# Gated attention in a two-block kernel: stacked halves of queries and keys, products with tokens on partitions, gates applied after the products

## What is computed

```python
def _masked_softmax(s, mask):
    s = jnp.where(mask, s.astype(jnp.float32), -1e30)
    m = jnp.max(s, axis=-1, keepdims=True)
    e = jnp.exp(s - m) * mask
    return e / jnp.maximum(jnp.sum(e, axis=-1, keepdims=True), 1e-30)

    # per block of 128 queries
        s = jnp.einsum('bqghd,bngd->bghqn', qb, k_cmp) * scale
        p_cmp = _masked_softmax(s - slopes * dist, dist >= 0)
        o_cmp = jnp.einsum('bghqn,bngd->bqghd', p_cmp.astype(v_cmp.dtype), v_cmp)
        ...
        s = jnp.einsum('bqghd,bgqmd->bghqm', qb, k_sel) * scale
        p = _masked_softmax(s - slopes * dist, dist >= 0)
        o_slc = jnp.einsum('bghqm,bgqmd->bqghd', p.astype(v_sel.dtype), v_sel)
        ...
        p = _masked_softmax(s - slopes * wd.astype(jnp.float32), wmask)
        o_win = jnp.einsum('bghqk,bkgd->bqghd', p.astype(vw.dtype), vw)
        o = gb[..., 0:1] * o_cmp + gb[..., 1:2] * o_slc + gb[..., 2:3] * o_win
```

## Times and profile before

| | |
|---|---|
| median of 3 runs | 2704.24 us (2703.32 to 2704.76) |
| the profiled execution | 2705.93 us, span 2704.1 us |
| PE busy | 2589.8 us, 96% of the span |
| DVE, ACT, POOL busy | 1299.0, 821.7, 1163.7 us |
| mean granted PE clock | 0.973 |
| first attention | about 190 to 492 us of the span |

### The profile page before, as it was taken

One profiled execution on the slowest core, in us unless ns is written; L12 is line 12 of the kernel. 1 busy time (PEld: TensorE's weight loads), 2 busy tenths in 40 slices (PEclk: granted clock), 3 DMA queues, 4 the chain that ended last, 5 costly groups with the idle time before them and its releaser, 6 DMA issues.

```text
span 2704.1 us, 37833 instructions
## 1 busy us (share of the span) xinstructions
PE 2589.8 (96%) x12935; PEld 2185.8 (81%) x12935; DVE 1299.0 (48%) x2419; ACT 821.7 (30%) x1458; POOL 1163.7 (43%) x564
## 2 busy tenths in 40 slices
PE   7969998899999999999999999999999999999998
PEld 5757877788788888789988888887899888888877
DVE  5578887566443222137776532221277765322211
ACT  2234555567321110024444321100144444211101
POOL 4742221000047777850000287778700001877786
PEclk8878998999999999999999999999999999999999
DMA  6320000233333333232223233333322232333332
GB/s 128 86 47 17 9 15 14 73 94 86 86 91 93 98 96 94 87 94 81 75 63 89 83 93 98 96 91 92 99 67 81 69 90 78 93 98 96 92 92 80
DMA packets 422924, 216.70 MB, mean 80 GB/s; under 512 B 59216, under 2 KB 422028, under 8 KB 422796
## 3 DMA queue, kind: packets, MB, share of 16 engines
q1 hardware_dynamic: 419836, 211.86, 27.5%
q10 hardware_dynamic: 2960, 3.22, 0.4%
HBM read 212.93 MB, written 2.10 MB: 80 GB/s over the span
## 4 chain that ended last, share of the span: by engine, by line
PE 81%; DVE 9%; ACT 4%; issue 3%; POOL 1%; SPq 1%; DMA 0%; ACTq 0%; DVEq 0%; POOLq 0%
PE psA L895 46%; PE psB L918 12%; PE psA L918 9%; PE psA L1119 5%; PE psB L1119 4%; PE psO L918 2%; ACT b L2168 1%; DVE b L1423 1%; DVE b L1446 1%; POOL b L665 1%; ACT b L2175 1%; PE psB L807 1%; DVE b L1749 1%; DVE b L1897 0%; DVE b L1442 0%
## 5 line engine op out<-in xcount | busy, mean ns | idle before, releaser
L895 PE MATMUL psA<-b,b 128*128 128x512 f32 (+1 forms) x5712 | 1307.2, 391 | 19.9 <-POOL b L665 10.5
L895 PEld LDWEIGHTS psA<-b,b 128*128 128x128 f32 x5712 | 1072.2, 190 | 253.7 <-POOL b L665 19.4
L663 POOL TENSOR_TENSOR b<-b,b 128x1024 fp32r<-128x1024 f32 x256 | 486.9, 1902 | 1285.5 <-PE psA L895 1098.8
L665 POOL TENSOR_TENSOR b<-b,b 128x1024 fp32r<-128x1024 f32 x256 | 633.2, 2473 | 20.1
L918 PE MATMUL psB<-b,b 128*128 128x512 f32 (+3 forms) x1914 | 429.4, 379 | 23.4 <-DVE b L1423 17.9
L918 PEld LDWEIGHTS psB<-b,b 128*128 128x128 f32 (+2 forms) x1914 | 345.7, 193 | 99.5 <-DVE b L1423 27.1
L918 PE MATMUL psA<-b,b 128*128 128x512 f32 (+1 forms) x1548 | 348.9, 380 | 11.2 <-DVE b L1402 11.2
L1258 DVE SCALAR_TENSOR_TENSOR b<-psA,b 128x512 f32<-128x512 f32 x152 | 104.7, 691 | 479.9 <-PE psA L895 473.8
L918 PEld LDWEIGHTS psA<-b,b 128*128 128x128 f32 x1548 | 276.1, 190 | 67.7 <-DVE b L1402 11.4
L1269 DVE TENSOR_TENSOR b<-b,psA 128x512 f32 x48 | 33.0, 688 | 346.1 <-PE psA L895 346.1
L2083 ACT ACTIVATE b<-b,b (+1 forms) x56 | 40.5, 724 | 453.0 <-DVE b L1269 446.6
(11 more groups left out here) (261 smaller groups left out, 2052.6 us busy)
## 6 DMA issues: line engine op xcount, KB each, us to landing
b<-in_w_in SPq DMA_DIRECT2D x296, 256.0 KB, 3.0
b<-in_w_ffn_in SPq DMA_DIRECT2D x176, 256.0 KB, 3.1
b<-in_w_ffn_out SPq DMA_DIRECT2D x64, 256.0 KB, 3.0
b<-in_w_out SPq DMA_DIRECT2D x48, 256.0 KB, 3.0
b<-in_w_gate SPq DMA_DIRECT2D x44, 256.0 KB, 3.1
b<-in_w_up SPq DMA_DIRECT2D x44, 256.0 KB, 3.2
b<-in_w_down SPq DMA_DIRECT2D x32, 256.0 KB, 3.0
b<-in_w_ffn_out SPq DMA_DIRECT2D x32, 192.0 KB, 2.5
```

The costliest lines, as they stand in the source:

```text
L663: nc.gpsimd.tensor_tensor(w[:, 0], wraw[:, s], ones[:, 0:1].broadcast_to([P, KT * P]), ALU.mult).then_inc(w_hi.sem, 1)
L665: nc.gpsimd.tensor_tensor(w[:, 1], wraw[:, s], hi_f(w[:, 0]), ALU.subtract).then_inc(w_lo.sem, 1)
L895: i = mm(dst, w[:, wh, kt, :], rhs(xh, kt), start=first and kt == 0 and n == 0, stop=last and kt == kts - 1 and n == 2)
```

## The change

- **Scores in two passes.** `qd` replaces `qz`: a head's queries stand in both halves of the partitions (`query_twice`: a DMA on SP copies them to the other half once `query_lo` is done). `ks` holds the keys' high part in one half and the low part in the other. Two passes (`two`) then give all of the product. The same holds for the compressed scores (`kc`). Each key norm now copies and subtracts in two halves of 64 partitions.
- **Sign and scale.** Gains of keys take the factor of the scale and a minus sign; maxima become minima, and DVE's negation per unit goes. The compressed mask goes: rows with no valid key are shifted by at most 1e28 (POOL, L743).
- **Products with tokens on partitions.** The transposed probabilities are the weights, and the values' high and low parts side by side (128 columns) the moving operand: 20 matmuls of 128 columns a unit. The first ten wait for `hi` alone.
- **Gates over sums applied to products.** The four scalings of `Pm` go. `scaled` (DVE) reads a unit's product from `psO`, multiplies by gate over sum and writes `ow`. `exps(U)` waits for `scaled(U-2)`.
- **Additions on POOL.** `head_added` adds two branches (512 columns), then the two value parts (256 columns), into `om`. `pair_output`, once a pair and one pair late, does three 512-wide matmuls of the compressed branch and four fp32 matmuls of `om` against the identity. One `out_hi` and one `out_lo` of 128 partitions per pair replace two of 64.
- **Moved to POOL:** the first norm factor (`query_root`), the compressed shift and scaling (`c_shift`, `c_scale`). The compressed biases leave POOL; DVE adds them (`c_biased`). The compressed scores of a pair now run in its own first unit, not a pair ahead.

The core of the diff:

```diff
+            def query_twice(n):
+                for hd in range(2):
+                    here, there = (slice(b * HD, (b + 1) * HD) for b in (hd, 1 - hd))
+                    sp.wait_ge(ql_pool.sem, ql_pool.at(n, f"lo{hd}"))
+                    sp.dma_start(hi_f(qd[there, hd, :, :]), hi_f(qd[here, hd, :, :])).then_inc(q_twice[hd], 16)
+            for n in range(4):
+                query_twice(n)
+                query_load(n + 4)
...
+            def head_added(j):
+                n, hd = j // 2, j % 2
+                pool.wait_ge(uo_dve.sem, uo_dve.at(2 * j + 1))
+                nc.gpsimd.tensor_tensor(ow[0][:, :], ow[0][:, :], ow[1][:, :], ALU.add).then_inc(oa_pool.sem, 1)
...
+                nc.gpsimd.tensor_tensor(om[:, :, hd, :], parts[:, :, 0, :], parts[:, :, 1, :], ALU.add).then_inc(oa_pool.sem, 1)
...
-                    three(psS[:, x % 2, 0:w], lambda h: qz[:, hd, h, qt * P:(qt + 1) * P],
-                          lambda h: kn[:, br, n // 4, h, 0:w], True, True).then_inc(us_pe.sem, 1)
+                    two(psS[:, x % 2, 0:w], lambda h: qd[:, hd, h, qt * P:(qt + 1) * P], ks[:, br, n // 4, hd, 0:w]).then_inc(us_pe.sem, 1)
...
+                for h in range(2):
+                    if h == 0:
+                        pe.wait_ge(uh_act.sem, uh_act.at(U))
+                    else:
+                        pe.wait_ge(ul_dve.sem, ul_dve.at(U))
+                    for qt in range(TT):
+                        for kt in range(qt + 1):
+                            at = PT_AT[kt] + (qt - kt) * P
+                            i = mm(psO[:, qt * P:(qt + 1) * P], PT[:, h, at:at + P],
+                                   vtok[:, br, kt, n // 4, hd, :, :].rearrange("p h d -> p (h d)"),
+                                   start=h == 0 and qt == 0, stop=h == 1 and kt == qt, skip_group_check=True)
...
+            def pair_output(n):
+                pe.wait_ge(cl_dve.sem, cl_dve.at(n))
+                pe.wait_ge(uo_dve.sem, uo_dve.at(4 * n + 4 if n < 7 else 31))
+                three(psO[:, :], lambda h: vc[:, h, n // 4, :], lambda h: PTc[h][:, :], True, False, True)
+                pe.wait_ge(oa_pool.sem, oa_pool.at(2 * n + 1))
+                for qt in range(TT):
+                    i = mm(psO[:, qt * P:(qt + 1) * P], om[:, qt, :, :].rearrange("p h d -> p (h d)"), ident,
+                           start=False, stop=qt == TT - 1, skip_group_check=True)
...
+            def scaled(U):
+                o = 32 * (U % 2)
+                dve.wait_ge(uv_pe.sem, uv_pe.at(U))
...
+                v.tensor_tensor(ow[U % 2][:, :].rearrange("p (q c) -> p q c", c=P), psO[:, :].rearrange("p (q c) -> p q c", c=P),
+                                st[:, o + 16:o + 20].unsqueeze(2).broadcast_to([P, TT, P]), ALU.mult).then_inc(uo_dve.sem, 1)
...
             def exps(U):
                 o = 32 * (U % 2)
-                act.wait_ge(um_dve.sem, um_dve.at(U))
-                for qt in range(TT):
+                if U >= 2:
+                    act.wait_ge(uo_dve.sem, uo_dve.at(U - 2))
+                for qt in reversed(range(TT)):
+                    act.wait_ge(um_dve.sem, um_dve.at(U, f"max{TT - 1 - qt}"))
```

More of the change, by code:

```diff
@@ L404, in build @@
         uv_pe = steps("unit_values", ["all"])
+        uo_dve = steps("unit_scaled", ["all"])
+        oa_pool = steps("head_added", ["units", "parts"])
         cs_pe = steps("compressed_scores", ["all"])
-        cm_dve = steps("compressed_maxima", ["add", "max", "sub"])
+        cm_dve = steps("compressed_maxima", ["add", "max"])
+        cs_pool = steps("compressed_shifted", ["floor", "all"])
         ce_act = steps("compressed_exps", ["exp"])
-        cp_dve = steps("compressed_probabilities", ["mask", "sum", "guard", "rec", "gate", "scale"])
+        cp_dve = steps("compressed_sums", ["sum", "guard", "rec", "gate"])
+        cp_pool = steps("compressed_probabilities", ["all"])
         ct_pe = steps("compressed_transposed", ["all"])
@@ L672, in _, with bias_of @@
                     split(i * RAW + s, i, s)
-            def bias_of(n, hd, c=False):
+            def bias_of(n, hd):
                 h = CONST["slope"].start + n + 8 * hd
[L678 to L689, removed]
+                dist = con[:, CONST["dist"]]
+                nc.gpsimd.tensor_tensor(bias[:, hd, :], dist, con[:, h:h + 1].broadcast_to(list(dist.shape)), ALU.mult).then_inc(b_pool.sem, 1)
@@ L857, in attention_pe, with unit @@
             pe.wait_ge(hn_dve.sem, hn_dve.at(4))
-            c_scores(0)
-            def unit(U, *beside):
+            def unit(U, first, then):
                 if U + 2 < 32:
@@ L865, in unit @@
                 transposes(U)
-                for f, *args in beside[:1]:
+                for f, *args in first:
                     f(*args)
@@ L869, in unit @@
                     scores(U + 2, (2, 3))
-                for f, *args in beside[1:]:
+                for f, *args in then:
                     f(*args)
@@ L1049, in compressed_norm @@
                 headnorm(4, blk, P)
-            attention_pe(pe, free, three, compressed, compressed_norm)
+            pair_output = attention_pe(pe, three, compressed, compressed_norm)
             def lru_proj(c, rhs=rhs_x):
@@ L1071, in _ @@
                     lru_proj(4 * m + x)
+                    if m == 0 and x == 0:
+                        pair_output(7)
                 if m == KT - 1:
@@ L1531, in _ @@
             dve.wait_ge(ql_pool.sem, ql_pool.at(0))
-            headnorm(4, kcraw[:, :], pcol("kg", 0), kc[:, 1], kc[:, 0], HD, P)
-            maxima(0, range(4))
-            maxima(1, range(4))
-            c_maxima(0)
-            probabilities(0)
-            c_probabilities(0)
+            low = slice(HD, P)
+            headnorm(4, kcraw[:, :], pcol("kg", 0), [("hi1", low, cols, kc[low, cols], kc[low, cols])
+                                                     for cols in (slice(0, HD), slice(HD, P))], HD, P)
+            maxima(0)
+            maxima(1)
             def weight_lo1(c):
```

385 lines of the change are left out of this document (212 added, 173 removed).

## The result

The changed kernel took 2712.15 us (median of 6 executions, 2706.75 to 2715.15), the kernel before 2704.23 in the executions beside it (2699.83 to 2705.73): ratio 1.0028, 95% interval 1.0017 to 1.0038. It is slower by 0.3%, 7.9 us, inside the stated range and 6 us above the forecast. The profiled executions differ by 8.5 us in span.

| stretch | before | after | difference | forecast |
|---|---|---|---|---|
| start to the norm sums of query 0 | 171.62 | 176.18 | +4.6 | +0.7 |
| from there to the first products | 35.3 | 28.3 | -7.0 | -8.5 |
| to the last products of pair 5 | 215.8 | 216.5 | +0.7 | +2.5 |
| to the last products of pair 7 | 66.4 | 73.0 | +6.6 | +4.9 |
| to the first LRU projection | 2.7 | 4.3 | +1.6 | 0 |

What follows compares the result with a forecast made beforehand. The first attention was taken as bound by its chain of waits, then by PE's clock. Terms 2.5 + 4.9 - 7.8 + 1 = +0.6, plus 1.5, gave 2704.2 + 2.1, 2706 us; range 2687 to 2718.

Steps and rivals of the forecast that it cites:

- The main case: First attention: the shorter chain's gain is given back by a lower clock, total 2706 us; chance 0.45.
- The place of the clock's cost: Low clock after unit 0's wait for `hi`: 1.7 us in unit 0, 2.2 in unit 1, 3.9 a pair.
- The reason given for the clock: Unit 0's compressed scores, 2.5 us wait for `hi` and narrow products are thin work, so the clock falls every pair.
- The four fp32 matmuls: Output matmuls against the identity on PE, once a pair: eight passes, 0.9 us, bounds 0.44 and 1.55.
- The DMA copy: Copied query for unit 2: ready after 10.1 us, hidden at 3.0 to landing; rival that it is late, 2714, chance 0.17.
- that rival: POOL holds DVE's gates before `lo`: 0.4 us a unit over 32 units, +13, 2719 us; chance 0.11.
- the last key norm gets a second copy and subtraction (+0.7): Start, before the first attention: doubled work of the last key norm adds 0.7 us.
- The start: From query 0's norm sums to the first products: -9.0 us from a shorter path, +0.5 for the copied query.
- the query pairs: Six pairs with query matmuls: 38.4 us each against 37.98, +0.4 each, +2.5 together.
- the last two pairs: Pairs without query matmuls: 33.8 and 29.5 us at full clock, 4 each for the clock; +1.9 and +3.0.
- the 1.5 I had added upward: Addition to the summed terms because the four fp32 matmuls and the gates lean upward: +1.5 us.
- a unit's exponentials now wait for `scaled` of two units before (they share the row sums): New wait entering the first attention's chain on ACT; steps of 7.4 us a unit plus ACT's work between.

Runs made afterwards that it cites:

- run 4: The changed kernel with 8 unused matmuls of 512 columns on PE ahead of unit 0's wait for `hi`; 2698.1 us, ratio 0.9973 to the kernel before.
- run 1: The changed kernel with ACT's roots of the next query moved ahead of the exponentials of the pair's second unit; 2703.2 us, ratio 0.9993 to the kernel before.
- run 2: The changed kernel with `query_hi` of head 0 ahead of `out_hi` on ACT in unit 1; 2707.2 us, ratio 1.0006 to the kernel before.
- run 7: The changed kernel with each key norm's parts written whole, 128 rows at once (scores compute something else); 2710.4 us, ratio 1.0021 to the kernel before.
- run 5: The changed kernel with exponentials waiting for the reciprocals of two units before instead of `scaled`; 2689.1 us, ratio 0.9942 to the kernel before.
- run 6: The changed kernel with early roots, `query_hi` ahead of `out_hi`, and exponentials waiting for the reciprocals; 2688.5 us, ratio 0.9936 to the kernel before.
- run 11: The changed kernel: exponentials waiting for reciprocals, `query_hi` first, compressed scores between product halves, unused matmuls in the last two pairs; 2688.5 us, ratio 0.9941 to before.

## Why the prediction came out as it did

**The main case held.** The chain got shorter, 34.36 us a pair at full clock where I had 34.5, and the clock took it back: 3.5 us a pair where I had 3.9 (run 4). The place of the clock's cost was right too: from run 4 to the change unit 0 grows by 1.7 us and unit 1 by 2.0, where I had 1.7 and 2.2. The low stretch behind `hi` lasted 6.8 to 10.2 us, where I had 8 or more in each pair. In the 34.36 two errors cancel, which was luck: units 0, 1 and 3 take 9.0, 8.3 and 7.6 us where I had 9.4, 8.7 and 8.0, and unit 2 takes 9.5 where I had 8.4, because of the copied query. The four fp32 matmuls do run as eight passes, (1.05-0.16) = 0.89 us in PE's timeline, for 0.9. Narrow products cost what the transposes' row said: (2.35-0.16)/20 = 0.110 us each at full clock, (4.50-0.2)/20 = 0.215 at half. The Trainium skill ("TensorE: Matmul & The Clock Gate", Back-to-back issue gap) gives about 81 ns for this width; the trace disagrees by a third, and the row decides.

**The reason given for the clock was in part wrong.** I called the stretch thin and listed the narrow matmuls beside the wait. Runs 1 and 4 show that at least half of the low time goes with the wait for `hi`: with it filled, a pair ran at 1.00 through thin scores and narrow products. In the changed kernel's pair the clock was back at 1.00 from 286.9 on, behind twenty narrow products, four score matmuls and ten transposes, and ahead of the query's wide matmuls at 288.62. The Trainium skill (the same page, HAM oscillation) ties the fall to long idle gaps of PE. By that nothing would have fallen here; the clock fell behind waits of 2.06 us, and in the kernel before behind 0.92, so the measurement decides. I had not read the kernel before to the end of the stage either. In two of its later pairs the clock fell behind the thin scores with no wait in front of the next scores, as here, where it is at 0.50 from 412.9 to 416.2 us:

```profile
410.22 2.87 PE L918 MATMUL psA<-b,b 128*128 128x32 f32 x24
412.93 1.52 PE L918 MATMUL psB<-b,b 128*128 128x256 f32 x6
414.25 3.01 PE L918 MATMUL psO<-b,b 128*128 128x512 f32 x12
```

What exactly brings the clock down, and how long it stays down, stays open.

**The DMA copy.** I let it be hidden at 3.0 us to landing. It took 3.15, but issued late: from the end of unit 0's products to PE's scores it took 294.17-282.83 = 11.3 us where I had 10.1, because `query_hi` stands behind `out_hi`, which waits for `pair_output`. That wait I had not put on the copy's path. Price: 1.2 us a pair (run 2).

**POOL and DVE.** Groups of the two gates in 221 to 411 us, the change and then the kernel before:

```profile
L1530 DVE TENSOR_TENSOR b<-b,b 128x4 f32<-128x4 f32 x20 | 5.5, 273 | 0.7
```

```profile
L1437 DVE TENSOR_TENSOR b<-b,b 128x4 f32<-128x4 f32 x20 | 9.7, 484 | 0.7
```

With more work on POOL the gate got shorter on average, and costs 0.1 us a unit over the undisturbed 0.16; its longest takes 1.01 us where it was 1.76. In these five pairs that rival didn't occur.

**Terms that were mis-sized.** The step "the last key norm gets a second copy and subtraction (+0.7)" failed: all four key norms get them, each waits for the one before through the shared buffers, and gates and compression stand behind on DVE. It was +4.6 in the profiled execution, 3.8 of which run 7 gave back at the norm sums; in the other runs that share this part the norm sums of query 0 come at 174.0 to 176.0 where the change's profiled execution has 176.18, so +2.4 to +4.6. The start gave 7.0 where I had 8.5, the query pairs +0.7 in place of +2.5, the last two pairs +6.6 in place of +4.9: PE waits for `hi` up to 3.5 us there and has no query to do, so the clock was at 0.74. The last unit's products at half clock (4.50 against 2.87) add 1.6, and the LRU begins at the low clock for another 2, where I had +1 for other reasons. With the late start the first products came at 204.44 us and not near 198. Less the 1.5 I had added upward the errors of these stretches come to +6.4, the distance of forecast and profiled execution.

**The chain's largest link I took as given.** I counted "a unit's exponentials now wait for `scaled` of two units before (they share the row sums)" as a cost of the change. Run 5 shows that it is a cost of one wait placed one step too late, and worth 23 us with what the clock gives back.

## What to carry to other kernels

When a change brings in a new wait, ask which reader it protects and wait for that one; here 66 us less DVE work bought no time while the exponentials waited for `scaled`, and the same kernel with the wait on its real reader is 16 us faster than the kernel before. Where PE's granted clock falls in every period of a loop, look for PE's waits and for sparse work around the fall, and either move what delays it (run 1) or, as a test that costs a few lines, fill it with matmuls nobody needs (run 4). Shortening a chain that leaves PE idle longer in one place can be paid back in clock, so look at PE's longest wait of a period beside the sum of its waits.

## What the runs showed that I had not expected

Work without use made the kernel faster: 8 matmuls of 512 columns in a wait of 2.06 us gave 14 us. Another 36 in the last two pairs took 6.9 us off those pairs in the profiled execution, but only 3.4 off the median, less than a measurement tells. The gains of runs 6 and 11 over run 5 in PE's waits did not show in the time, at a granted clock of 0.92 and 0.93 for 0.94; why is not settled. And one wait on ACT, which the change itself had brought in, cost about three times what the change as a whole lost.
